# Attention inputs of a decoder trunk on one core: from stationary weight tiles to token-major rows with moving weights, in nine blocks

## The chip, the cores and the metric

The kernel runs on one core of one Trainium2 chip. A core has TensorE (matrix products, from SBUF into PSUM), VectorE (DVE in the rows), ScalarE (ACT), GpSimd (POOL), SyncE (SP, here the issuer of nearly all loads) and 16 DMA engines. The time is that of the device for one execution, in microseconds (us); the number compared is the median over runs.

## The reference

One batch of 256 tokens, model width 2048, two layers: a sparse-attention mixer and a short convolution, each followed by a SwiGLU FFN (hidden width 5632). All is fp32. The change lies in the first mixer:

```python
def _dsa_mixer(h, w_in, q_norm, k_norm, w_out):
    proj = h @ w_in                       # columns: q 2048, k 512, v 512, qi 1024, ki 64, wi 16
    q, k, v, qi, ki, wi = jnp.split(proj, ATTN_SPLITS, axis=-1)
    ...
    q = _rope(_rmsnorm(q, q_norm), cos_h, sin_h)      # 16 heads of 128
    k = _rope(_rmsnorm(k, k_norm), cos_h, sin_h)      # 4 heads of 128
    qi = _rope(qi, cos_i, sin_i)                      # 16 index heads of 64
    ki = _rope(ki, cos_i, sin_i)[:, :, 0, :]
    ...
    rel = jax.nn.relu(jnp.einsum('bqhd,bsd->bqhs', qi_b, ki).astype(jnp.float32))
    idx_score = jnp.einsum('bqhs,bqh->bqs', rel, wi_b.astype(jnp.float32))
    idx_score = jnp.where(causal, idx_score, -jnp.inf)
    _, sel = lax.top_k(idx_score, topk)               # 64 keys of each query
    ...                                               # softmax over the selected keys, grouped heads
    return o @ w_out
```

`h` is the RMS norm of x over the 2048 columns. The rotation of a head takes its halves x1 and x2 to x1 cos - x2 sin and x2 cos + x1 sin, with angles by token position.

## The kernel before

**Precision and slots.** Each fp32 matrix is split into a high part (rounded to the fp32r type) and a low rest, and a product is the sum high x high + high x low + low x high. Weights come in slots of 128 x 1024 numbers: SP loads a slot into `stage`, ScalarE copies it to `w_hi` (L1006), VectorE subtracts to get `w_lo` (L1393), TensorE uses both. `w_hi` and `w_lo` hold four slots (RING), so ScalarE may split slot n once TensorE has finished slot n-4. In the attention part `stage` is used four deep too, later eight deep (DEEP). Normed activations lie token-last in `xs` (and `hs` for head outputs and FFN hiddens): 128 features on partitions, 256 tokens, high then low.

**Order.** There is no scheduler: each engine has a program of its own, written slot by slot, and after certain slots come extra steps (the dictionaries `{slot: [steps]}`; `steps_between` walks them). Engines meet only by semaphores. An engine takes its instructions in order, so a step that waits holds up the weight splits behind it.

**Attention inputs.** Function `stream` keeps a 128x128 weight tile stationary and moves `xs`: the high tile against high and low activations (512 columns, L520), the low tile against the high ones (256 columns, L525). The result is feature-major: 128 features on partitions, 256 tokens in two halves of a bank, which ScalarE and VectorE add (`take_cross` L1012, `qkv_sum` L1594) and scale by the token's norm, broadcast over partitions (L1596). The stages:
- the first block: x arrives in four column parts, is transposed on TensorE (`turn_x`, L584), and the index key with the head weights (80 columns) and the first 256 index columns are multiplied along with it;
- three index blocks of 256 columns. A rotation of halves is a product with a constant matrix on TensorE (`qi_turn` L628, `ki_turn` L614 to L617); scores are L640, their sums over heads L1551, then eight rounds of top-8 and replace on VectorE (L1567, L1570);
- four groups g, each with k and v of one kv head (four slots) and its four query heads (eight slots). On TensorE `turn_kvq` has the mean of k squared (L668), the rotation of k (L670), the turn of v (L672) and the rotation of two query heads (L676); `turn_q23` the other two (L683); `vars_q` sixteen products with one column (L692) for the mean squares of the queries. GpSimd multiplies by the cosine (`cos_products`, L1981 and L1983), VectorE by the sine (L1601, L1613) and adds. Then come logits (L702), softmax (exps L1162, `normalise` L1644), turns of the probabilities (L711) and outputs (L717 to L722), in the next group.

**Output projection.** `stream_rows` (L549 to L551) moves the weights, 512 columns, against stationary 128x128 tiles of `hs`: the result is token-major. Four blocks j of eight slots; each is added to the residual `res`, and the steps of the next norm run between the slots (`norm_steps`). The head-3 group's logits, softmax and outputs run in the first block. The FFN that follows (L774 to L776) and all after it use the same slot machinery; there GpSimd issues DMAs that add one weight block to another (L1994).

## Time and profile before

| | us |
|---|---|
| median of 3 runs | 2097.96 |
| lowest, highest | 2097.86, 2098.32 |
| the profiled execution, from its first to its last instruction (span) | 2096.4 |
| TensorE busy | 2081.3 (99%) |
| VectorE busy | 1725.3 (82%) |
| ScalarE busy | 1177.2 (56%) |
| GpSimd busy | 118.3 (6%) |
| first weight product starts | 13.2 |
| first product of the FFN starts | 349.4 |

The profile is one execution, taken by the hardware. Its own time is the span of 2096.4 us with 1.6 us around it, against the median. A row of a timeline gives start and duration of one or several like instructions; products overlap, so TensorE's pace is read from the distance between starts and not from the duration. "PE" is TensorE's products, "PEld" its weight loads, which run beside them. "a <- b" is the tile written and the tiles read. A wait names the engine that ended it.

### The profile page before, as it was taken

How to read it: one execution, taken by the hardware profiler on the slowest of the kernel's cores; microseconds unless marked ns; L12 is line 12 of the kernel's file. 1: busy time of each engine (PE TensorE's matmuls, PEld its weight loads, DVE VectorE, ACT ScalarE, POOL GpSimd, SP SyncE). 2: the span in 40 equal slices, each digit the busy share in tenths (PEclk: the TensorE clock that was granted, in tenths of full speed). 3: DMA queues.
4: the chain of work that ended last, by engine and by line, in shares of the span. 5: the costliest groups of instructions: out<-in, count | busy, mean ns of one | idle time of the engine just before them, and what ended most of it. 6: DMA issues, size and time to landing. Idle time of an engine off the chain costs nothing.

```text
span 2096.4 us, 28772 instructions
## 1 busy us (share of the span) xinstructions
PE 2081.3 (99%) x9675; PEld 1729.7 (83%) x9675; DVE 1725.3 (82%) x1968; ACT 1177.2 (56%) x1428; POOL 118.3 (6%) x131
## 2 busy tenths in 40 slices
PE   8999999999999999999999999999999999999999
PEld 7888878788888888888888888888888888888887
DVE  5887757999999997876788877579999999978666
ACT  5456555665566564554465555466655665645443
POOL 0001000001000000000000000000010000000000
PEclk9999999999999999999999999999999999999999
DMA  7555456777777777667667666567777777767674
GB/s 230 152 145 152 158 171 192 223 224 227 228 226 220 231 219 215 216 202 215 211 196 211 204 203 196 190 196 222 224 226 229 225 221 230 221 213 216 204 220 147
DMA packets 251616, 432.33 MB, mean 206 GB/s; under 512 B 16912, under 2 KB 58000, under 8 KB 251536
## 3 DMA queue, kind: packets, MB, share of 16 engines
q1 hardware_dynamic: 233824, 399.23, 58.8%
q0 software_dynamic: 16848, 30.68, 8.7%
q10 hardware_dynamic: 864, 1.37, 0.2%
q8 instruction: 49, 0.80, 0.2%
q14 instruction: 31, 0.25, 0.0%
HBM read 429.12 MB, written 2.10 MB: 206 GB/s over the span
## 4 chain that ended last, share of the span: by engine, by line
PE 96%; DVE 2%; ACT 1%; issue 1%; DMA 0%; ACTq 0%; DVEq 0%; SPq 0%
PE ps L774 24%; PE ps L776 24%; PE ps L775 24%; PE ps L520 6%; PE ps L551 4%; PE ps L549 4%; PE ps L550 4%; PE ps L525 3%; PE ps L584 2%; DVE w_lo L1393 1%; PE ps L702 0%; PE ps L640 0%; ACT w_hi L1006 0%; PE ps L711 0%; PE ps L692 0%
## 5 line engine op out<-in xcount | busy, mean ns | idle before, releaser
L1393 DVE TENSOR_TENSOR w_lo<-stage,w_hi 128x1024 fp32r<-128x1024 f32 x748 | 902.3, 1222 | 232.4 <-ACT w_hi L1006 228.4
L1006 ACT ACTIVATE w_hi<-stage 128x1024 fp32r<-128x1024 f32 x748 | 772.7, 1055 | 536.6 <-PE ps L776 365.5
L774 PE MATMUL ps<-w_hi,xs 128*128 128x512 f32 x1122 | 439.4, 392 | 0.3
L776 PE MATMUL ps<-w_hi,xs 128*128 128x512 f32 x1122 | 437.0, 389 | 0.0
L775 PE MATMUL ps<-w_lo,xs 128*128 128x512 f32 x1122 | 436.6, 389 | 0.0
L774 PEld LDWEIGHTS ps<-w_hi,xs 128*128 128x128 f32 x1122 | 210.6, 188 | 44.3 <-DVE gated L1699 1.1
L776 PEld LDWEIGHTS ps<-w_hi,xs 128*128 128x128 f32 x1122 | 210.6, 188 | 44.1
L775 PEld LDWEIGHTS ps<-w_lo,xs 128*128 128x128 f32 x1122 | 210.7, 188 | 42.9
L774 PE MATMUL ps<-w_hi,hs 128*128 128x512 f32 x584 | 227.6, 390 | 0.0
L776 PE MATMUL ps<-w_hi,hs 128*128 128x512 f32 x584 | 227.2, 389 | 0.0
L775 PE MATMUL ps<-w_lo,hs 128*128 128x512 f32 x584 | 227.2, 389 | 0.0
L520 PE MATMUL ps<-xs,w_hi 128*128 128x512 f32 (+1 forms) x528 | 170.7, 406 | 0.0
L1246 ACT ACTIVATE t_hi<-t_raw 128x1024 fp32r<-128x1024 f32 x117 | 123.8, 1058 | 76.3 <-DVE t_raw L1735 45.2
L1742 DVE TENSOR_TENSOR t_lo<-t_raw,t_hi 128x1024 fp32r<-128x1024 f32 x117 | 142.9, 1222 | 17.5 <-ACT t_hi L1246 17.5
L1735 DVE TENSOR_TENSOR t_raw<-stage,t_raw 128x1024 f32<-128x1024 f32 x117 | 142.7, 1220 | 0.0
L1994 POOL DMA_DIRECT2D stage<-in_w_gate x86 | 75.7, 881 | 1034.1 <-DMA stage<-in_w_up 833.5
L776 PEld LDWEIGHTS ps<-w_hi,hs 128*128 128x128 f32 x584 | 109.6, 188 | 22.8
L774 PEld LDWEIGHTS ps<-w_hi,hs 128*128 128x128 f32 x584 | 109.6, 188 | 22.7
L775 PEld LDWEIGHTS ps<-w_lo,hs 128*128 128x128 f32 x584 | 109.6, 188 | 22.5
L1242 ACT ACTIVATE t_hi<-t_raw 128x512 fp32r<-128x512 f32 x117 | 73.4, 627 | 95.3 <-PE ps L776 67.2
L525 PEld LDWEIGHTS ps<-xs,w_lo 128*128 128x128 f32 (+1 forms) x528 | 96.8, 188 | 21.4
L525 PE MATMUL ps<-xs,w_lo 128*128 128x256 f32 (+1 forms) x528 | 103.2, 280 | 0.0
(226 smaller groups left out, 2824.7 us busy)
## 6 DMA issues: line engine op xcount, KB each, us to landing
stage<-in_w_gate SPq DMA_DIRECT2D x176, 512.0 KB, 4.0
stage<-in_w_up SPq DMA_DIRECT2D x176, 512.0 KB, 4.9
stage<-in_w_down SPq DMA_DIRECT2D x176, 512.0 KB, 4.9
stage<-in_conv_w_in SPq DMA_DIRECT2D x96, 512.0 KB, 4.8
stage<-in_attn_w_in SPq DMA_DIRECT2D x48, 512.0 KB, 3.8
stage<-in_w_gate POOLq DMA_DIRECT2D x86, 256.0 KB, 5.6
stage<-in_attn_w_out SPq DMA_DIRECT2D x32, 512.0 KB, 4.8
stage<-in_conv_w_out SPq DMA_DIRECT2D x32, 512.0 KB, 4.8
```

The source lines that it names most:

```text
L520: return pe.matmul(ps[0:count, banks[m], :], w_hi[:, slot, at], rhs, start=k == 0, stop=last)
L525: return pe.matmul(ps[0:count, banks[m], TOK:], w_lo[:, slot, at], rhs[:, 0:TOK], start=False, stop=False)
L549: pe.matmul(bank, hi, w_hi[:, slot, cols], start=k == 0, stop=False)
L550: pe.matmul(bank, hi, w_lo[:, slot, cols], start=False, stop=False)
L774: pe.matmul(ps[:, bank, :], hi, b_hi, start=start, stop=False)
L775: pe.matmul(ps[:, bank, :], hi, b_lo, start=False, stop=False)
L776: return pe.matmul(ps[:, bank, :], lo, b_hi, start=False, stop=stop)
L1006: nc.scalar.activation(w_hi[:, j % RING, :], stage[:, at, :], ACT.Copy).then_inc(hi_done, 1)
L1246: nc.scalar.activation(t_hi[:, 0:2, :], t_raw[:, 0:2, :], ACT.Copy).then_inc(t_high, 1)
L1393: tt(w_lo[:, p, :], stage[:, stage_at(first + j), :], f32(w_hi[:, p, :]), ALU.subtract).then_inc(lo_done, 1)
L1735: tt(t_raw[:, 0:2, :], left, bcast(t_raw[:, 2, :], 2), ALU.subtract).then_inc(t_step, 1)
L1742: tt(t_lo[:, 0:2, :], t_raw[:, 0:2, :], f32(t_hi[:, 0:2, :]), ALU.subtract).then_inc(t_ready, 1)
```

## The change

The attention inputs are computed token-major, in nine blocks of eight slots (`FRONT`): block 0 has the last four index heads, the index key and the head weights (336 columns), blocks 1 and 2 six index heads each (384), block 3 all of k, block 4 all of v, blocks 5 to 8 four query heads each (512). A slot has 256 rows of a block. The 128x128 activation tiles are stationary and the weights move, six products per 128 rows.

- The norm's factor is one number per token and partition, applied by ScalarE as it evicts a block into `rows` (`evict`).
- Rotation on rows: GpSimd multiplies by the cosine table (`cos`), VectorE multiplies the swapped halves by the signed sine table (`swap`), and VectorE (index blocks, `index_add`) or GpSimd (k and q, `head_add`) adds. The head norms' gains are multiplied into the tables once, on GpSimd (`head_tables`). k is scaled by its inverse norm on GpSimd.
- Mean squares of heads come from ScalarE's squares with an accumulator (`head_squares`, eight small ones for each of k and the four query blocks).
- Each rotated block is transposed on TensorE (`index_turn`, `turn_k`, `turn_q`) and copied out by ScalarE. v needs no turn.
- The matrices for means and rotations go; the tables are token-major, and their five loads are issued by GpSimd after the last part of x.
- `stage` is eight deep throughout, x comes in five parts, a table load for ScalarE stands at the start, and the loops over blocks are written out.
- In the output projection the slots of the first two column blocks are interleaved (`AO_SLOTS`), so that rows of late heads come late, and the norm steps move with it.

GpSimd's queue before, from its first product to the loop's end (`s_made`, `k_gained`, `q_gained` are semaphores of TensorE and ScalarE):

```order
L1981 TENSOR_TENSOR kr<-k_gn,tab 128x256 [waits k_gained,in_small]
L1983 TENSOR_TENSOR qr<-gated,tab 128x1024 [waits q_gained]
L1985 UNCONDITIONAL_BRANCH
L1985 ISA
L1980 REGISTER_ALU [waits k_gained]
L1981 TENSOR_TENSOR kr<-k_gn,tab 128x256 [waits s_made]
L1982 REGISTER_ALU
L1983 TENSOR_TENSOR qr<-gated,tab 128x1024 [waits q_gained]
```

GpSimd's queue in the changed kernel, up to the first query block's sum (`sums` and `cross` are the buffers of the rotated rows and of the swapped products; `front_taken` is an eviction, `index_turned` and `k_turned` are TensorE's turns):

```order
L1920 TENSOR_TENSOR sums<-rows,tab_i 128x2x320 [waits front_taken,in_small]
L1905 TENSOR_TENSOR tab_k<-tab_h,hgain 128x256 x2
L1905 TENSOR_TENSOR tab_q<-tab_h,hgain 128x256 x2
L1920 TENSOR_TENSOR sums<-rows,tab_i 128x2x384 [waits index_turned,front_taken] x2
L1920 TENSOR_TENSOR sums<-rows,tab_k 128x1024 [waits index_turned,front_taken,tab_made]
L1927 TENSOR_TENSOR sums<-sums,cross 128x1024 [waits front_swapped,front_cos]
L1940 TENSOR_TENSOR sums<-sums,k_inv 128x1024 [waits front_roped,k_inverse]
L1920 TENSOR_TENSOR sums<-rows,tab_q 128x1024 [waits k_turned,front_taken]
L1927 TENSOR_TENSOR sums<-sums,cross 128x1024 [waits front_swapped,front_cos]
```

What was four pairs of products became eight products over the blocks, four for the tables, five sums and one scaling; each waits for an eviction or a turn, and TensorE's turns wait for them.

TensorE before, at the end of a head group and where the next begins:

```order
L668 MATMUL ps<-k_sq,mat_a 128x256 [waits k_squared,rel_done]
L670 MATMUL ps<-k_gn,mat_a 128x256 [waits k_gained]
L672 MATMUL ps<-mat,raw 128x128 x2
L676 MATMUL ps<-gated,mat_a 128x256 [waits q_gained]
L676 MATMUL ps<-gated,mat_a 128x256
```

TensorE in the changed kernel, in block 6 after its third slot, where the first query block is turned (`mat` is the identity):

```order
L584 MATMUL ps<-w_lo,xs 128x512
L585 MATMUL ps<-w_hi,xs 128x512
L618 MATMUL ps<-mat,sums 128x128 [waits kr_ready,front_roped]
L618 MATMUL ps<-mat,sums 128x128 x7
L583 MATMUL ps<-w_hi,xs 128x512 [waits lo_done]
```

The means and rotations by constant matrices are gone; one wait on the summed rows, and eight turns, stand in the place of a group's matrix work.

VectorE in the changed kernel, second and third block, around the first index turn's input:

```order
L1480 TENSOR_TENSOR cross<-rows,tab_i 128x2x5x32 [waits in_small,front_taken]
L1480 TENSOR_TENSOR cross<-rows,tab_i 128x2x5x32
L1360 TENSOR_TENSOR w_lo<-stage,w_hi 128x768 [waits hi_done] x2
L1488 TENSOR_TENSOR sums<-sums,cross 128x2x320 [waits front_swapped,front_cos]
L1491 COPY sums<-sums 128x2x64 [waits front_roped]
L1360 TENSOR_TENSOR w_lo<-stage,w_hi 128x768 [waits hi_done] x3
```

The copy ends what TensorE's first index turn waits for; two weight splits stand ahead of the sum.

The code, cut to what the steps below speak of:

```diff
+FRONT = ((D + 2 * KV * HD + 12 * ID, 4 * ID + ID + IH), (D + 2 * KV * HD, 6 * ID), (D + 2 * KV * HD + 6 * ID, 6 * ID),
+         (D, KV * HD), (D + KV * HD, KV * HD), *((g * REP * HD, REP * HD) for g in range(KV)))
+KI_AT = 4 * ID
+WI_AT = KI_AT + ID
+K_BLOCK, V_BLOCK, Q_BLOCK = 3, 4, 5
+FRONT_SLOTS = KT // 2
+
+S_AO = len(FRONT) * FRONT_SLOTS
+AO_SLOTS = (*((j, s) for j in range(2) for s in range(4)), *((j, s) for j in range(2) for s in range(4, 6)),
+            *((j, s) for j in range(2) for s in range(6, 8)), *((j, s) for j in range(2, 4) for s in range(8)))
+AO_DONE = tuple(S_AO + AO_SLOTS.index((j, FRONT_SLOTS - 1)) + 1 for j in range(4))
+AO_NORM = (14, 18, 24)
...
+            sp.dma_start(mat.ap(), ident).then_inc(in_ident, 16)
+            load_x(x_part(0), in_x[0])
+            load_front(0, 0)
+            load_x(x_part(1), in_x[1])
+            load_front(0, 1)
+            for j in range(1, 4):
+                load_x(slice(WIDE * j, WIDE * (j + 1)), in_x[j + 1])
+                load_front(0, 2 * j)
+                load_front(0, 2 * j + 1)
+            for b in range(1, len(FRONT)):
+                for s in range(FRONT_SLOTS):
+                    load_front(b, s)
+            for at, (j, s) in enumerate(AO_SLOTS):
+                load(S_AO + at, at % DEEP, attn_w_out[s * 2 * P:(s + 1) * 2 * P, WIDE * j:WIDE * (j + 1)], WIDE)
 
             def load_wide(first, w, tiles):
...
+            def front_slot(b, s):
+
+                width = FRONT[b][1]
+                slot = s % RING
+                if s == 0 and b >= 2:
+                    pe.wait_ge(front_taken, 2 * (b - 1))
+                if b == 0:
+                    x_low_done(pe, s)
+                pe.wait_ge(lo_done, FRONT_SLOTS * b + s + 1)
+                for kk in range(2):
+                    k = 2 * s + kk
+                    cols = slice(kk * width, (kk + 1) * width)
+                    for a in range(2):
+                        bank = ps[:, FRONT_BANKS[b % 2][a], 0:width]
+                        hi, lo = half(xs, k, a)
+                        pe.matmul(bank, hi, w_hi[:, slot, cols], start=k == 0, stop=False)
+                        pe.matmul(bank, hi, w_lo[:, slot, cols], start=False, stop=False)
+                        mm = pe.matmul(bank, lo, w_hi[:, slot, cols], start=False, stop=k == KT - 1)
+                mm.then_inc(slot_used, 1)
+
...
+            def index_turn(b):
+
+                if b == 0:
+                    pe.wait_ge(index_added, 1)
+                else:
+                    pe.wait_ge(front_roped, b + 1)
+                    pe.wait_ge(rel_done, b)
+                for m in range(3):
+                    for a in range(2):
+                        at = TOK * (m % 2) + P * a
+                        mm = pe.transpose(ps[:, 6 + m // 2, at:at + P], roped[:, a, P * m:P * (m + 1)], IDENT)
+                mm.then_inc(index_turned, 1)
...
+            steps = {(1, 4): [lambda: index_turn(0)], (1, 6): [lambda: score_heads(0)],
+                     (2, 3): [lambda: index_turn(1)], (2, 5): [lambda: score_heads(1)],
+                     (3, 3): [lambda: index_turn(2)], (3, 5): [lambda: score_heads(2)],
+                     (3, 7): [lambda: score_heads(3)], (4, 5): [turn_k]}
+            for p in range(KV):
+                at = Q_BLOCK + 1 + p
+                steps = merged(steps, {(at, 2): [lambda p=p: turn_q(p)], (at, 3): [lambda p=p: logits(p)],
+                                       (at + 1, 0): [lambda p=p: turn_prob(p)], (at + 1, 1): [lambda p=p: outputs(p)]})
+            for h in range(3):
+                turn_x(h)
+            for b in range(len(FRONT)):
...
+            def evict(b):
+
+                act.wait_ge(slot_used, FRONT_SLOTS * (b + 1))
+                if b == 0:
+                    act.wait_ge(first_rs, 1)
+                elif b != V_BLOCK:
+                    act.wait_ge(front_swapped, rope_no(b))
+                    act.wait_ge(front_cos, rope_no(b))
+                dst = v_rows if b == V_BLOCK else rows
+                for a in range(2):
+                    nc.scalar.activation(dst[:, a, 0:FRONT[b][1]], ps[:, FRONT_BANKS[b % 2][a], 0:FRONT[b][1]],
+                                         ACT.Copy, scale=rs[:, 0, a:a + 1]).then_inc(front_taken, 1)
+
+            def head_weights():
...
+            steps = {(1, 0): [lambda: x_square(0, 0)], (1, 1): [lambda: x_square(0, 1)],
+                     (1, 2): [lambda: x_square(1, 0)], (1, 3): [lambda: x_square(1, 1)],
+                     (1, 4): [first_root_step], (1, 5): [lambda: evict(0), head_weights],
+                     (2, 0): [lambda: index_copy(0)], (2, 2): [lambda: relu(0)], (2, 3): [lambda: evict(1)],
+                     (2, 7): [lambda: index_copy(1)], (3, 1): [lambda: relu(1)], (3, 3): [lambda: evict(2)],
+                     (3, 7): [lambda: index_copy(2)], (4, 1): [lambda: relu(2)],
+                     (4, 3): [lambda: evict(K_BLOCK)], (4, 4): [lambda: relu(3), k_squares], (4, 5): [root_k],
+                     (5, 1): [copy_k], (5, 3): [lambda: evict(V_BLOCK)]}
+            for p in range(KV):
+                at = Q_BLOCK + 1 + p
+                steps = merged(steps, {(at, 3): [lambda p=p: evict(Q_BLOCK + p)], (at, 4): [lambda p=p: q_squares(p)],
+                                       (at, 5): [lambda p=p: root_q(p)], (at, 6): [lambda p=p: copy_q(p)],
+                                       (at + 1, 0): [lambda p=p: exps(p, 0)], (at + 1, 1): [lambda p=p: exps(p, 1)],
...
+            def swap(b):
+
+                dve.wait_ge(front_taken, 2 * b + 2)
+                if b == 0:
+                    dve.wait_ge(in_small, 80)
+                elif b == K_BLOCK:
+                    dve.wait_ge(tab_made, 4)
+                if rope_no(b):
+                    dve.wait_ge(front_roped, rope_no(b))
+                if b == 1:
+                    dve.wait_ge(index_added, 1)
+                dim = rope_heads(b)[1]
+                src = by_head(rows, b)
+                dst = by_head(swapped, b)
+                sin = rope_table(b)[:, 1, :, :]
+                for side in range(2):
+                    to, of = (slice(dim // 2 * s, dim // 2 * (s + 1)) for s in (side, 1 - side))
...
+            steps = {(1, 0): [set_score], (1, 3): [first_sum], (1, 4): [first_scale], (1, 5): [lambda: swap(0)],
+                     (1, 7): [lambda: index_add(0)], (2, 2): [lambda: add_scores(0)], (2, 3): [lambda: swap(1)],
+                     (2, 5): [lambda: index_add(1)], (3, 1): [lambda: add_scores(1)], (3, 3): [lambda: swap(2)],
+                     (3, 5): [lambda: index_add(2)], (4, 1): [lambda: add_scores(2)], (4, 3): [lambda: swap(K_BLOCK)],
+                     (4, 4): [lambda: add_scores(3), bound_scores], (4, 5): [invert_k],
+                     (4, 7): [lambda: top_rounds((0,))]}
+            steps = merged(steps, {(5, j): [lambda j=j: top_rounds((j + 1,))] for j in range(7)}, {(5, 7): [make_mask]})
+            for p in range(KV):
+                at = Q_BLOCK + 1 + p
+                steps = merged(steps, {(at, 3): [lambda p=p: swap(Q_BLOCK + p)], (at, 7): [lambda p=p: logit(p)],
+                                       (at + 1, 1): [lambda p=p: normalise(p, 0)],
...
+            pool.wait_ge(in_x[4], 16)
+            for dst, src in ((tab_i, tables_i), (tab_h, tables_h), (hgain, head_gains), (bound, bounds), (taps, conv_taps)):
...
+            cos(0)
+            head_tables(tab_k, 2)
+            head_tables(tab_q, 0)
+            cos(1)
+            cos(2)
+            pool.wait_ge(tab_made, 4)
+            cos(K_BLOCK)
+            head_add(K_BLOCK)
+            pool.wait_ge(k_inverse, 1)
+            pool.wait_ge(front_roped, rope_no(K_BLOCK) + 1)
+            inverse = k_inv[:, :, :].unsqueeze(3).to_broadcast([P, 2, KV, HD])
+            nc.gpsimd.tensor_tensor(by_head(roped, K_BLOCK), by_head(roped, K_BLOCK), inverse, ALU.mult).then_inc(k_ready, 1)
+            for p in range(KV):
+                cos(Q_BLOCK + p)
+                head_add(Q_BLOCK + p)
 
```

## Rows read from the trace of the kernel before

**Rows 1.** The page, part 4: the chain that ended last, by engine.
```profile
PE 96%; DVE 2%; ACT 1%; issue 1%; DMA 0%; ACTq 0%; DVEq 0%; SPq 0%
```

**Rows 2.** Windows of three stages, us; the first line names the columns.
```profile
core 0: us, PE busy (x) PEld busy (x) DVE busy (x) ACT busy (x) POOL busy (x), PEclk, DMA share, GB/s
13.20:32.50 19.30, 19.30 (x108) 16.00 (x106) 11.59 (x21) 14.92 (x28) 0.00 (x0) 0.91 0.83 247
...
74.10:248.10 174.00, 173.64 (x1008) 149.00 (x1006) 134.47 (x223) 100.38 (x161) 12.66 (x7) 1.00 0.52 154
248.10:349.40 101.30, 99.75 (x464) 81.99 (x463) 67.29 (x81) 57.33 (x90) 3.39 (x2) 1.00 0.53 169
```

**Rows 3.** Waits of TensorE in 0 to 350 us: total, times, longest.
```profile
PE ps L584 <- DMA res<-in_x: 6.3, 1, 6.3
PE ps L584 <- DVE xs L1418: 2.4, 1, 2.4
PE ps L711 <- DVE prob L1644: 1.4, 1, 1.4
```

**Rows 4.** The start: chain, timeline (start, length), DMA rate to 30 us.
```profile
1.33 4.85 DMA res<-in_x
...
8.34 1.28 ACT L1032 ACT_TABLE_LOAD   x1 [8.34 <-PE ps L584]
...
13.22 0.67 PE L520 MATMUL ps<-xs,w_hi 128*80 128x512 f32 x1
...
GB/s 0 0 89 165 210 218 292 374 335 364 397 370 361 324 339 363 378 412 389 415 399 343 300 319 333 316 331 231 141 341 253 41 191 365 175 270 322 105 232 330
```

**Rows 5.** Timeline of TensorE: products of a head group, then of the projection.
```profile
205.81 0.62 PE L520 MATMUL ps<-xs,w_hi 128*128 128x512 f32 x2
206.27 0.40 PE L525 MATMUL ps<-xs,w_lo 128*128 128x256 f32 x2
206.50 0.63 PE L520 MATMUL ps<-xs,w_hi 128*128 128x512 f32 x2
...
262.92 0.39 PE L551 MATMUL ps<-w_hi,hs 128*128 128x512 f32 x1
263.15 0.39 PE L549 MATMUL ps<-w_hi,hs 128*128 128x512 f32 x1
```

**Rows 6.** The chain of 0 to 360 us in order: small groups.
```profile
56.77 0.87 PE ps L628 x4
...
209.45 0.87 PE ps L683 x4
210.32 1.68 PE ps L692 x16
...
289.75 0.87 PE ps L584 x8
```

**Rows 7.** Timelines of GpSimd (three rows) and of VectorE (two).
```profile
103.59 0.74 POOL L1981 TENSOR_TENSOR kr<-k_gn,tab 128x256 f32<-128x256 f32 x1 [102.58 <-ACT k_gn L1127]
117.77 3.41 POOL L1983 TENSOR_TENSOR qr<-gated,tab 128x1024 f32<-128x1024 f32 x1 [13.44 <-ACT gated L1140]
...
162.92 2.39 POOL L1983 TENSOR_TENSOR qr<-gated,tab 128x1024 f32<-128x1024 f32 x1 [12.88 <-ACT gated L1140]
...
163.75 1.84 DVE L1605 TENSOR_TENSOR kr<-kr,k_sq 128x256 f32<-128x256 f32 x1
165.63 0.42 DVE L1608 TENSOR_TENSOR kr<-kr,k_rt 128x256 f32<-128x256 f32 x1
```

**Rows 8.** Timeline of ScalarE: first exp, and the split after the eighth.
```profile
136.42 0.40 ACT L1162 ACTIVATE prob<-prob,npeak 128x128 f32<-128x128 f32 x1
...
139.95 2.00 ACT L1006 ACTIVATE w_hi<-stage 128x1024 fp32r<-128x1024 f32 x2
```

**Rows 9.** The page, parts 5 and 6: GpSimd DMA issues and landing.
```profile
L1994 POOL DMA_DIRECT2D stage<-in_w_gate x86 | 75.7, 881 | 1034.1 <-DMA stage<-in_w_up 833.5
...
stage<-in_w_gate POOLq DMA_DIRECT2D x86, 256.0 KB, 5.6
```

885 lines of the change are left out of this document (351 added, 534 removed).

## The prediction

> **What bounds the kernel now.** I read the chain that ended last first: 96% of it is TensorE [rows 1]. So time goes only where TensorE's own work gets shorter, or a wait of TensorE goes; what VectorE, ScalarE, GpSimd or the DMAs save is worth nothing by itself. The second view is the table of stages [rows 2]. The change touches the stretch from 0 to 349.4 us: the first block (13.2 to 32.5), the index blocks (to 74.1), the four head groups (to 248.1) and the output projection (to 349.4). What follows, 1747 us, runs the same instructions. The third is TensorE's waits [rows 3]: 8.7 us at the start; behind it TensorE is idle for 174.0 - 173.64 = 0.4 us in the head groups and 101.3 - 99.75 = 1.5 in the projection [rows 2], 1.9 in all. DMA is at half to two thirds of its share in the stretch, the clock at its full level after the first block [rows 2]. The whole sum is therefore one over TensorE's queue from 0 to 349.4 us, plus the waits that the new order makes.
>
> **Start.** Today the first weight product starts at 13.2 us [rows 4]. Ahead of it stand the landing of x's first 512 KB (1.33 + 4.85 us), 16 turns of x (two column blocks), a table load of 1.28 us on ScalarE that nothing hides, and the splits. Afterwards the table is loaded ahead, and x's first part is halved. But TensorE's queue holds three turns of x ahead of the first product, and the third needs the second column block, behind 64 + 256 + 344 + 256 + 344 + 512 KB = 1.78 MB. With 0.58 MB ahead, the first 512 KB landed at 6.2 us; 1.2 MB more at 0.3 to 0.37 MB per us (row of GB/s) is 9.4 to 10.2 us. Four turns follow, about 0.8 us (at most twice their later 0.11 each): first product at 10.3 us, **-2.9 us** (from -4.5, if data comes faster, to -1).
>
> **Weight products.** Today one 128x128 weight tile costs a 512- and a 256-column product. Four of these (two tiles) start every 0.69 to 0.70 us, 0.349 us a tile [rows 5]; 33 tiles (the 80-column one costs the same) times 16 rows are 184.3 us. Afterwards the weights move: per 128 rows and block six products of the block's width. A 512-column product is shown in the output projection: 0.2275 us from start to start [rows 5]; six blocks of 96 are 576 x 0.2275 = 131.0 us. Widths 384 and 336 no row shows. The nearest are 512 (0.2275) and 256 (0.116, half of the 0.23 that a pair of low products takes); on the line between them they are 0.172 and 0.151 us: 192 x 0.172 + 96 x 0.151 = 47.5 us. Bounds: no gain from narrowness (0.2275 each) is +18 us, strictly by columns without the 0.005 us of offset -1. I take the line, since 256 and 512 lie on it. Sum 178.5: **-5.8 us**. It is small, as the columns streamed are nearly the same.
>
> **Small products.** These lie on TensorE in full, and here the gain is [rows 6]. Gone: four rotations of index queries (L628, 0.87 each, 3.5), the index key (two products of that size and two turns, 1.1) and the statistic (two of half the size, 0.4); in each of four head groups the key's mean and rotation (two products as in L628, 0.86, so 3.4), the value's two turns (0.9 in all), the query rotations (L676 as L683, 0.86 each, 6.9) and the means of the squares (L692, 1.68, so 6.7). Together 23.0 us. Added: 18 index turns and 40 head turns; a turn is 0.109 us (L584, eight in 0.87): 6.3 us. Scores, logits, probability turns and outputs stay. Twelve more turns of x fall behind the first product: +1.3. **-15.4 us**. Of the 349.4 us, the parts priced here and those that stay leave some 3 us over; I put it on the 33 places where TensorE turns from small groups back to weights, 0.1 us each. 24 places remain: **-1.0 us** (0 to -2).
>
> **The output projection.** 32 slots before and after, same products. Reordering lets eight slots run before head 2's output is needed and twelve before head 3's. Today logits, softmax and outputs of the last heads leave the 1.5 us of idle, nearly all in one wait of 1.4 [rows 3]. ScalarE's and VectorE's norm steps move from slots 12 to 18. Slot 16 then waits for an addition that VectorE makes behind split 17; it has slots 14 and 15, 5.4 us, for two splits and 1.2 us of sum. Worth nothing beyond the waits below.
>
> **New waits: the term that decides.** Weight splits on ScalarE (1.06) and VectorE (1.22, for 1024 elements) stand in the same in-order queues as the steps, and may run three slots ahead of TensorE. A turn after slot n that needs a step queued behind split n+3 has one slot (2.06 us at width 384) for split, split and step.
> - First index turn: it stands after slot 4 of the second block, its sum on VectorE behind split 7. Split 0.8, split 0.95, sum and copy 1.1 = 2.9 against 2.06: 0.8 us late, always.
> - In this place GpSimd makes a product and four tables. Today's rows show what it does to VectorE [rows 7]: the sum of two SBUF operands took 1.84 us in place of 0.42 while GpSimd's product ran, to 0.3 us past its end, and another such product took 3.41 in place of 2.39. So they exclude each other. Four tables of 0.74 us can each slip between VectorE's splits: up to +3.0. I take +2.2, since not all of them meet the four operations in question.
> - Second index turn: two slots of lead, but 3.3 us of score sums and GpSimd's 1.8 us product in them: 0.9. Third: two wide slots, 0.
> - Key turn: ScalarE's eviction, eight squares, root, then GpSimd's 2.4 us scaling, in six slots: 0.5. First query turn: eviction (split 1.06, 1.1), two GpSimd products of 2.39 [rows 7] with a 1.3 us VectorE product between them, 7.2 against 8.2 us; any one exclusion overdraws it: 0.7. Later ones have 3.5 us more, from the probability turns and outputs in between.
> - Per head: ScalarE needs 8 splits (8.5), an eviction 1.1, exps 3.5 (eight from 136.42 to 139.95), squares as many and at most as much, two tables 2.6 [rows 4, 8], copies 1.1 + 1.6 + 1.1 (1024, 1536 and 1024 elements at a split's rate) and a root 0.3, together 23.3 us in a block where TensorE has 8 x 2.73 + 7 = 29 us. Probability turns are due 0.5 to 0.9 us after their input is ready, query copies 1.2 us: 1.0 for all four.
> Together 0.8 + 2.2 + 0.9 + 0.5 + 0.7 + 1.0 = 6.1, in place of 1.9: **+4.2 us**. The bounds are 0 to 20 us in all.
>
> On the exclusion, the Trainium skill has the rule: SBUF — State Buffer, section "SBUF: two separate sides", calls the shared port pair an exclusive lock held for a whole instruction, against a VectorE instruction with two SBUF inputs. The trace agrees by the 1.84 us. The rule speaks against this change, which brings GpSimd from 8 products to 18. If it held up every one of these behind VectorE's splits, on top of the waits above, it would be the second rival's time.
>
> **Sum.** -2.9 - 5.8 - 15.4 - 1.0 + 4.2 = **-20.9 us**. The profiled execution's span is 2096.4, its own median 2097.96, so 1.56 us lie around the span and stay. 2096.4 - 20.9 = 2075.5 of span, **2077 us**.
>
> **Rivals.**
> 1. All steps are covered: waits of 1 us in place of 6.1, and a start at 9.5 us: 2071. For it: VectorE is free for a third of the stretch [rows 2]. Against: the first turn's 0.8 us is in the order. 15%.
> 2. GpSimd and VectorE hold each other up: ten more operations of 2.4 us, of which each costs half on a chain with no slack, +12 us: 2089. For it: 3.41 and 1.84 [rows 7]. Against: most have 2 to 4 us of slack. 14%.
> 3. Constants late: GpSimd now issues the five constant loads behind the last part of x, which lands about 16 us; issues of 0.9 and a landing of 5.6 [rows 9] put them at 26 us, against first need at 35. If instead they go one by one, 16 + 5 x 6.5 = 48 us, and the first index turn waits 11 us: 2088. No row shows two loads in flight on that queue. 8%.
> 4. Widths 384 and 336 cost as 512: +18 us, 2095, within 0.2%. 4%.
> 5. Slower: ScalarE becomes the bound of the head blocks. Its in-order queue puts each head's squares, copies and exps between splits; it decides above 29 us a block. If squares and exps cost their two records without overlap and each step waits a slot, it is 23.3 + 11.2 = 34.5 us (sixteen records of 0.19 us, and four waits of half a slot and more), 5.5 us more in each of the blocks with head work (five), on top of 6: 2077 + 27 = 2104. Against: exps overlap today [rows 8]. 6%.
> 6. The end of the projection collides with the FFN's start, +4: 2081, inside the forecast's own range.
>
> **How the numbers follow.** Forecast 53% (2073 to 2083), rivals 1 to 5 15, 14, 8, 4 and 6%. The range leaves out the slower case and the top of rival 4: 2068 to 2092. Faster by over 0.2% (4.2 us, about what can be told from no change): forecast, rivals 1, 2, 3 = 0.90; same 0.04; slower 0.06.
>
> **What would show it.** The first product at 10 us; first FFN product at 328 us in place of 349.4; 512-column products 0.2275 us apart throughout; a wait of about 3 us ahead of the first index turn, named VectorE, and under 1 us elsewhere; GpSimd's 1024-element products above 2.4 us. Wrong would be a wait at every head, idle ScalarE waiting for loads, or a stage beyond 350 us that changes its length.

## The result and the profile after

The changed kernel takes **2078.02 us** by the median (four runs, 2075.32 to 2079.43) against 2098.0 for the kernel before (2097.86 to 2098.32). The ratio is 0.9903, with a 95% interval of 0.9889 to 0.9917. The profiled execution has a span of 2077.5 us and took 2079.43; the two runs next to the median had spans of 2076.0 and 2076.2. TensorE is still 96% of the chain that ended last. The first FFN product starts at 330.55 us, where it was 349.42, so 18.87 us are gone ahead of it. Behind it lie 1746.95 us, as before (1746.98).

Windows of the changed kernel: the first block, blocks 1 and 2, blocks 3 to 8 with the projection's first four slots, and the rest of the projection. The columns are those of [rows 2].

```profile
10.48:29.45 18.97, 18.97 (x118) 18.86 (x117) 12.06 (x21) 12.79 (x25) 2.90 (x5) 1.00 0.94 328
29.45:73.52 44.07, 41.39 (x238) 39.68 (x237) 29.01 (x41) 23.15 (x31) 11.26 (x6) 0.92 0.58 191
73.52:245.79 172.27, 171.15 (x812) 139.28 (x812) 135.77 (x193) 109.25 (x226) 37.01 (x12) 1.00 0.49 161
245.79:330.55 84.76, 84.76 (x390) 69.67 (x389) 54.06 (x68) 49.21 (x79) 1.28 (x2) 1.00 0.53 169
```

Behind the first block DMA, VectorE and ScalarE are as far from full as before (in it the DMA share is 0.94, where [rows 2] had 0.83); the granted clock of the second window is 0.92, where [rows 2] had 1.00 behind the first block. That is the first thing that the forecast did not have. TensorE's waits up to 330 us (total, times, longest), in answer to [rows 3]:

```profile
PE ps L549 <- DMA res<-in_x: 7.5, 3, 4.4
PE ps L598 <- DVE sums L1491: 2.7, 1, 2.7
PE ps L618 <- POOL sums L1927: 1.1, 1, 1.1
```

Behind the start there are two, 2.7 us ahead of the first index turn and 1.1 us ahead of the first query turn. The wait of 1.4 us ahead of the probability turns is gone.

TensorE's timeline at the start, then pairs of neighbouring products of 336, 384 and 512 columns, in answer to [rows 4, 5]:

```profile
9.72 1.12 PE L549 MATMUL ps<-mat,res 128*128 128x128 f32 x4 [1.96 <-DMA res<-in_x]
10.48 0.63 PE L583 MATMUL ps<-w_hi,xs 128*128 128x336 f32 x1
10.91 0.48 PE L584 MATMUL ps<-w_lo,xs 128*128 128x336 f32 x1
11.19 0.48 PE L585 MATMUL ps<-w_hi,xs 128*128 128x336 f32 x1
...
15.22 0.32 PE L583 MATMUL ps<-w_hi,xs 128*128 128x336 f32 x1
15.37 0.32 PE L584 MATMUL ps<-w_lo,xs 128*128 128x336 f32 x1
...
37.94 0.33 PE L584 MATMUL ps<-w_lo,xs 128*128 128x384 f32 x1
38.12 0.33 PE L585 MATMUL ps<-w_hi,xs 128*128 128x384 f32 x1
...
76.97 0.39 PE L583 MATMUL ps<-w_hi,xs 128*128 128x512 f32 x1
77.19 0.39 PE L584 MATMUL ps<-w_lo,xs 128*128 128x512 f32 x1
```

The first product comes at 10.48 us. The pace, from start to start, is 0.28 us at first, and later 0.15 for 336 columns, 0.17 for 384 and 0.23 for 512 (the mean over neighbouring products of a width at full pace is 0.154, 0.174 and 0.227). The chain's groups of six index turns and eight key turns, in answer to [rows 6]:

```profile
84.61 0.66 PE ps L598 x6
...
116.27 0.88 PE ps L618 x8
```

Around the first index turn (VectorE, then GpSimd, then TensorE):

```profile
35.62 2.27 DVE L1480 TENSOR_TENSOR cross<-rows,tab_i 128x320 f32<-128x320 f32 x2
37.81 2.90 DVE L1360 TENSOR_TENSOR w_lo<-stage,w_hi 128x768 fp32r<-128x768 f32 x2
40.64 1.34 DVE L1488 TENSOR_TENSOR sums<-sums,cross 128x640 f32<-128x640 f32 x1
42.01 0.63 DVE L1491 COPY sums<-sums 128x128 f32<-128x128 f32 x1
```

```profile
35.74 1.81 POOL L1920 TENSOR_TENSOR sums<-rows,tab_i 128x640 f32<-128x640 f32 x1 [11.62 <-ACT rows L1046]
37.50 2.40 POOL L1905 TENSOR_TENSOR tab_k<-tab_h,hgain 128x256 f32<-128x256 f32 x2
39.86 2.70 POOL L1905 TENSOR_TENSOR tab_q<-tab_h,hgain 128x256 f32<-128x256 f32 x2
```

```profile
42.70 1.54 PE L598 MATMUL ps<-mat,sums 128*128 128x128 f32 x6 [2.68 <-DVE sums L1491]
43.89 0.67 PE L583 MATMUL ps<-w_hi,xs 128*128 128x384 f32 x1
44.36 0.52 PE L584 MATMUL ps<-w_lo,xs 128*128 128x384 f32 x1
44.68 0.52 PE L585 MATMUL ps<-w_hi,xs 128*128 128x384 f32 x1
...
49.00 0.34 PE L584 MATMUL ps<-w_lo,xs 128*128 128x384 f32 x1
49.18 0.34 PE L585 MATMUL ps<-w_hi,xs 128*128 128x384 f32 x1
```

TensorE has slot 4's last product at 39.68 us. The sum of the rotated rows ends at 42.0 and its copy at 42.6. VectorE's four operations ahead of the turn (two splits, the sum, the copy) all lie beside GpSimd's tables (37.5 to 42.6 us). And behind the turn the products of 384 columns are 0.32 us apart, up to 48.7 us; then they are 0.17 to 0.18 apart again.

The first query turn's input, VectorE's swap and GpSimd's product and sum:

```profile
146.73 3.50 DVE L1480 TENSOR_TENSOR cross<-rows,tab_q 128x512 f32<-128x512 f32 x2
...
146.78 2.91 POOL L1920 TENSOR_TENSOR sums<-rows,tab_q 128x1024 f32<-128x1024 f32 x1 [32.23 <-ACT rows L1046]
150.38 3.23 POOL L1927 TENSOR_TENSOR sums<-sums,cross 128x1024 f32<-128x1024 f32 x1 [0.69 <-DVE cross L1480]
```

The two start together and take 3.50 and 2.91 us, where the swap takes 1.28 by itself (all_four, at 142.58 us) and GpSimd's product of this size took 2.39 [rows 7]. The sum, which comes to GpSimd while VectorE is at a split, takes 3.23 us.

### The profile page after: what moved, and what is told of

Read it like the earlier page. It is cut to its first block, busy times and chain, and to the rows that moved or that the text cites. A ratio compares the mean times of both kernels' runs of the same rounds, so it can differ in the third digit from the quotient of the medians.

```text
span 2077.5 us, 27665 instructions
## 1 busy us (share of the span) xinstructions
PE 2061.7 (99%) x9395; PEld 1713.1 (82%) x9395; DVE 1708.2 (82%) x1914; ACT 1178.1 (57%) x1487; POOL 154.4 (7%) x146
## 4 chain that ended last, share of the span: by engine, by line
PE 96%; DVE 2%; ACT 1%; issue 1%; DMA 0%; POOL 0%; SPq 0%; ACTq 0%; DVEq 0%; POOLq 0%
PE ps L723 24%; PE ps L724 24%; PE ps L725 24%; PE ps L523 3%; PE ps L521 3%; PE ps L522 3%; PE ps L583 3%; PE ps L585 3%; PE ps L584 3%; PE ps L537 2%; PE ps L687 1%; PE ps L688 1%; PE ps L689 1%; PE ps L642 1%; DVE w_lo L1347 0%
## 5 line engine op out<-in xcount | busy, mean ns | idle before, releaser
L1347 DVE TENSOR_TENSOR w_lo<-stage,w_hi 128x1024 fp32r<-128x1024 f32 x688 | 832.0, 1223 | 224.2 <-ACT w_hi L952 220.6
L952 ACT ACTIVATE w_hi<-stage 128x1024 fp32r<-128x1024 f32 x688 | 710.0, 1054 | 491.6 <-PE ps L725 364.7
L1360 DVE TENSOR_TENSOR w_lo<-stage,w_hi 128x1024 fp32r<-128x1024 f32 (+2 forms) x72 | 89.4, 1246 | 42.7 <-ACT w_hi L1008 42.5
L583 PE MATMUL ps<-w_hi,xs 128*128 128x512 f32 (+2 forms) x288 | 111.2, 386 | 0.0
L1008 ACT ACTIVATE w_hi<-stage 128x1024 fp32r<-128x1024 f32 (+2 forms) x72 | 70.3, 977 | 69.2 <-PE ps L585 69.1
```

The costliest lines, as they stand in the source:

```text
L583: pe.matmul(bank, hi, w_hi[:, slot, cols], start=k == 0, stop=False)
L952: nc.scalar.activation(w_hi[:, j % RING, :], stage[:, at, :], ACT.Copy).then_inc(hi_done, 1)
L1347: tt(w_lo[:, p, :], stage[:, stage_at(first + j), :], f32(w_hi[:, p, :]), ALU.subtract).then_inc(lo_done, 1)
L1360: tt(w_lo[:, p, 0:w], stage[:, stage_at(n), 0:w], f32(w_hi[:, p, 0:w]), ALU.subtract).then_inc(lo_done, 1)
```

## Experiments

after_again is the changed kernel once more, the other eleven are edits of it; each was timed in five rounds beside the kernel before. "TensorE's stretch" is from its first weight product to its first FFN product in the profiled execution; it leaves out the start and what lies behind. "Low" is how long TensorE ran at the lower pace from the first index turn on. The kernel before was timed 30 times in these rounds and lay between 2096.32 and 2099.19: it scatters by 2.9 us too, more than its first four runs showed.

| kernel | median us | lowest to highest | stretch us | wait, index turn | low us | wait, query turn |
|---|---|---|---|---|---|---|
| changed | 2078.02 | 2075.32 to 2079.43 | 320.07 | 2.7 | 6.0 | 1.1 |
| after_again | 2078.01 | 2075.70 to 2079.50 | 318.62 | 2.7 | 2.9 | 1.1 |
| tables_first | 2074.79 | 2074.31 to 2075.10 | 315.18 | 1.0 | 0 | 1.1 |
| turn_later | 2074.23 | 2073.84 to 2074.41 | 314.81 | 0.6 | 0 | 1.1 |
| start_two | 2076.63 | 2075.32 to 2076.75 | 319.47 | 2.7 | 2.9 | 1.1 |
| all_four | 2072.70 | 2071.89 to 2073.23 | 315.89 | 0 | 0 | 1.3 |
| add_on_vector | 2075.18 | 2074.22 to 2076.62 | 317.67 | 2.7 | 3.1 | 0 |
| turn_sooner | 2080.55 | 2079.98 to 2081.34 | 321.75 | 4.7 | 5.8 | 1.1 |
| turns_twice | 2080.29 | 2079.95 to 2082.64 | 321.16 | 2.7 | 0 | 1.1 |
| joined_vector | 2069.91 | 2069.31 to 2071.03 | 312.57 | 0 | 0 | 0 |
| joined_early | 2071.17 | 2071.05 to 2072.17 | 313.90 | 0 | 0 | 0 |
| ao_short | 2077.35 | 2077.13 to 2079.68 | 318.38 | 2.7 | 0 | 1.1 |
| joined_twice | 2075.16 | 2074.11 to 2075.57 | 317.94 | 0 | 0 | 0 |

**The changed kernel once more.**

> The changed kernel once more, as the yardstick of this set and to see its scatter: its four times so far lie from 2075.3 to 2079.4 us where the kernel before keeps within 0.5 us. Theory (clock): the wait of 2.7 us ahead of the first index turn is at the edge of what lets the granted clock fall to its lower level, and the products behind it (43.9 to 48.8 us) run at 0.32 us in place of 0.174. Then the time is about 2078 with a scatter of some us. Rival: the scatter was chance, and it is 2078 within 0.5.

The median is the same and so is the scatter: eight runs within 4.2 us. One row each of the granted clock, over 6.0 us from the first index turn on: the changed kernel, this repetition, and turns_twice, which does up to this place the same instructions:

```profile
42.70:48.70 6.00, 6.00 (x21) 6.00 (x22) 0.81 (x1) 1.33 (x2) 0.00 (x0) 0.50 0.27 100
```

```profile
42.70:48.70 6.00, 5.94 (x29) 5.94 (x30) 1.57 (x3) 1.66 (x2) 0.00 (x0) 0.76 0.31 112
```

```profile
42.00:48.00 6.00, 5.97 (x43) 5.68 (x45) 1.80 (x2) 2.49 (x3) 0.00 (x0) 1.00 0.32 115
```

PEclk (the number behind the five engines) is 0.50, 0.76 and 1.00. In the first, TensorE ran at 1.2 GHz for all of the 6.0 us; in the second for half of it; in the third not at all. The wait ahead was 2.68 us in all three. So one and the same wait lets the clock fall or not from run to run, and for a different time. At 0.32 us in place of 0.174 a product, 6.0 us at the lower level cost 2.8 us. From the first index turn to the second the first takes 19.96 us, the second 18.43 and the third 17.12, for the same instructions: the low clock cost 2.8, 1.3 and 0 us. The spans of the first two differ by the same 1.5 us (2077.5 and 2076.0): the scatter between these two is the clock's.

**Tables ahead of the first product.**

```diff
-            cos(0)
             head_tables(tab_k, 2)
             head_tables(tab_q, 0)
+            cos(0)
```

> GpSimd makes its four head tables ahead of its first cosine product, in its idle time from 29 to 35.7 us, and not between the two blocks' products. Theory (exclusion, then clock): VectorE's split, sum and copy behind the first swap (1.49, 1.28 and 0.64 us beside the tables) fall to about 0.96, 0.8 and 0.3; the wait ahead of the first index turn falls from 2.7 to 1.3 us, the clock stays at its upper level, and with it some 2.7 us of slow turns and products go: about 2074. Rival 1 (the order alone makes the wait): the wait stays at 2.7 and the time at 2078. Rival 2 (shorter wait, but the clock falls as before): 2076.5.

VectorE's last operations ahead of the turn, and TensorE's wait:

```profile
38.01 1.81 DVE L1360 TENSOR_TENSOR w_lo<-stage,w_hi 128x768 fp32r<-128x768 f32 x2
39.75 0.81 DVE L1488 TENSOR_TENSOR sums<-sums,cross 128x640 f32<-128x640 f32 x1
40.59 0.23 DVE L1491 COPY sums<-sums 128x128 f32<-128x128 f32 x1
...
PE ps L598 <- DVE sums L1491: 1.0, 1, 1.0
```

Two splits 1.81 us (2.90 beside the tables), sum 0.81 (1.34), copy 0.23 (0.63): 2.0 us less for the same four instructions, while the swap beside the cosine product stays at 2.28. The wait is 1.0 us and the clock stays at its upper level. The median falls by 3.2 us: 1.7 of wait, the rest clock. The theory of the exclusion holds in size (I had put 2.2 us of the wait on it), and the two rivals, that the order alone makes the wait and that the clock falls all the same, do not.

**The first index turn one slot later.**

```diff
-            steps = {(1, 4): [lambda: index_turn(0)], (1, 6): [lambda: score_heads(0)],
+            steps = {(1, 5): [lambda: index_turn(0)], (1, 6): [lambda: score_heads(0)],
```

> TensorE makes the first index turn after slot 5 of the second block in place of slot 4; nothing else changes. Theory: TensorE fills 2.08 us with the slot's products, the wait falls from 2.7 to 0.6 us and the clock stays up: 2.1 + 2.7 = 4.8 us less, about 2073, and the scatter of the changed kernel goes. Rival (the wait only moves: the split of the slot behind it is late too, since ScalarE stands at the copy of the turn): no gain, 2078. Rival 2 (the low clock is no result of the wait): the wait falls, 12 products at 0.32 us stay, 2076.

```profile
PE ps L598 <- DVE sums L1491: 0.6, 1, 0.6
```

A wait of 0.6 us is left of 2.7 (the slot fills 2.1), no product runs slow, and the median is 3.8 us lower. The four runs lie within 0.6 us, where the changed kernel's lie within 4. Of two separate ways to shorten the wait both give more than the wait itself, and both end the scatter.

**The first index turn one slot sooner.**

```diff
-            steps = {(1, 4): [lambda: index_turn(0)], (1, 6): [lambda: score_heads(0)],
+            steps = {(1, 3): [lambda: index_turn(0)], (1, 6): [lambda: score_heads(0)],
```

> The first index turn one slot sooner, after slot 3 of the second block, which makes the wait ahead of it longer by one slot's products: 2.7 + 2.1 = 4.8 us. Theory (an idle stretch of that size lets the granted clock fall, once, for a stretch whose length varies from run to run by some 3 us and doesn't grow with the wait): 2080.1, scatter as in the changed kernel. Rival (the low clock grows with the idle time): slow products for 8 us and more, 2082 or more. Rival 2 (the wait ends no later, since the sum behind split 7 needs that slot's end): under 0.5 us.

```profile
PE ps L598 <- DVE sums L1491: 4.7, 1, 4.7
```

The wait is 4.7 us and the time 2080.55, by 2.5 us longer where the theory had 2.1. The products of 384 columns that are 0.32 us apart are no more than in the changed kernel's profile, fourteen against fifteen. All five runs lie within 1.4 us, as if all had the penalty; only one of them was profiled. Over all profiles here the clock fell behind the wait of 4.7 us (one profile), behind that of 2.7 us in four of six, and behind one of 1.4 us or less never, the first block left aside.

**Two turns of x ahead of the first slot.**

```diff
-            for h in range(3):
+            for h in range(2):
                 turn_x(h)
...
-                    if b == 0 and s + 3 < 8:
-                        turn_x(s + 3)
+                    if b == 0:
+                        for h in ((2, 3) if s == 0 else (s + 3,)):
+                            if h < 8:
+                                turn_x(h)
```

> Two turns of x stand ahead of the first slot in place of three; turns three and four follow behind that slot. Theory (the start is the landing of x's third part at 9.7 us and no wait for weights): the first product comes at 8.2 us in place of 10.5, the later parts land long before their use, and the saving stays: 2.3 us less, about 2075.7. Rival 1 (the load queue sets the block's pace: what starts earlier waits later for loads or for ScalarE's copies): under 0.5 us. Rival 2 (the engine starts cold and the idle stretch behind it grows): nothing or a loss of 1 us.

```profile
8.57 0.62 PE L583 MATMUL ps<-w_hi,xs 128*128 128x336 f32 x1 [0.52 <-DVE w_lo L1362]
...
12.07 1.91 PE L549 MATMUL ps<-mat,res 128*128 128x128 f32 x8
13.63 0.50 PE L583 MATMUL ps<-w_hi,xs 128*128 128x336 f32 x1
```

The first product comes at 8.57 us, 1.9 earlier. The new wait of 0.5 us stands directly ahead of it: without the third turn in between, TensorE comes to the first slot before VectorE has split its weights (until 8.4 us). And the third turn is moved, not saved: turns three and four take 1.56 us behind the first slot, at the lower clock, where the fourth alone took 0.69 in the changed kernel. Against after_again, whose clock was low as long behind the index turn, the first FFN product comes 1.0 us earlier; by the medians 1.4 us are left of the 2.3 that I expected. No load was late, so rival 1 is wrong about the cause and the theory was wrong about the size.

**Four edits at once.** The three edits that gained, and this one:

```diff
-                steps = merged(steps, {(at, 3): [lambda p=p: evict(Q_BLOCK + p)], (at, 4): [lambda p=p: q_squares(p)],
+                steps = merged(steps, {(at, 2): [lambda p=p: evict(Q_BLOCK + p)], (at, 4): [lambda p=p: q_squares(p)],
```

> Four edits to the changed kernel at once: tables ahead of the first cosine product, the first index turn after slot 5, two turns of x ahead of the first slot, and ScalarE evicts each query block after split 2 of the next block in place of split 3 (the eviction stands ahead of that split). Theory (each removes its own part of TensorE's idle time): the index wait and the slow products behind it go in full (-4.4 us from 2078.0), the start gives 1.4 as it did alone, the wait of 1.1 us ahead of the first query turn goes: 2071. Rival (the edits collide: an eviction ahead of its split holds up the weights, or the block with the tables comes earlier than its constants): 2073 or more, with a wait of TensorE for w_lo or for the tables.

GpSimd's cosine product and VectorE's split in block 6, and two waits of TensorE:

```profile
139.17 2.40 POOL L1922 TENSOR_TENSOR sums<-rows,tab_q 128x1024 f32<-128x1024 f32 x1 [31.18 <-ACT rows L1048]
...
140.07 2.58 DVE L1362 TENSOR_TENSOR w_lo<-stage,w_hi 128x1024 fp32r<-128x1024 f32 x1 [2.59 <-ACT w_hi L1010]
...
PE ps L618 <- POOL sums L1929: 1.3, 1, 1.3
PE ps L583 <- DVE w_lo L1362: 0.9, 1, 0.9
```

The first two edits take away the same wait and the same low clock, so their gains don't add. All four together give 5.3 us, where 4.4 and 1.4 us were expected of the first three. The fourth gives nothing, and shows the exclusion once more: GpSimd's product runs from 139.17 to 141.57 us, and the split that comes to VectorE at 140.07 ends at 142.65, after 2.58 us in place of 1.23. That is 1.08 us behind the product's end: nearly the whole split stood still until GpSimd was through. The swap waits behind it. The other wait, 0.9 us, stands ahead of the very first product (at 8.30 us), as in start_two.

**The query sums on VectorE.** In `dve` the sum stands behind the swap, in `pool` it goes:

```diff
-                steps = merged(steps, {(at, 3): [lambda p=p: swap(Q_BLOCK + p)], (at, 7): [lambda p=p: logit(p)],
+                steps = merged(steps, {(at, 3): [lambda p=p: swap(Q_BLOCK + p), lambda p=p: query_add(p)], (at, 7): [lambda p=p: logit(p)],
...
                 cos(Q_BLOCK + p)
-                head_add(Q_BLOCK + p)
```

> VectorE makes the sums of the four query blocks right behind its swapped products; GpSimd keeps the cosine products and the key block. Theory (only the first query turn was late, and GpSimd's sum of 3.23 us beside VectorE's split was its cause): the wait of 1.1 us goes, 2076.9; the other blocks had slack and give nothing. Rival (VectorE is the tighter queue; its logits and prob steps come later): new waits of TensorE ahead of the probability turns, 2079 or more.

```profile
PE ps L549 <- DMA res<-in_x: 7.2, 3, 4.4
PE ps L598 <- DVE sums L1491: 2.7, 1, 2.7
```

These are all of TensorE's waits up to 300 us. The query wait is gone and none came in its place. The median is 2.8 us lower, more than 1.1; but this profile's clock was low for 3.1 us and the changed kernel's for 6.0, so the medians of two scattered kernels can't tell the 1.1 from the rest. Against after_again (2.9 us of low clock) TensorE's stretch is 0.95 us shorter, about the wait that is gone.

**Turns twice.**

```diff
-                for h in range(4):
+                for h in (0, 1, 2, 3, 0, 1, 2, 3):
```

> Every turn of a key or query block is made twice (40 turns more, to the same place). It measures the term on which the forecast rests, that small groups lie on TensorE in full and at 0.109 us a turn. Theory: 40 x 0.109 = 4.4 us more, 2082.4. Rival (they lie beside waits that would be there anyway): under 1 us, save for the block with the wait.

The key turns of this kernel, then those of the changed one:

```profile
112.61 1.91 PE L618 MATMUL ps<-mat,sums 128*128 128x128 f32 x16
```

```profile
116.11 1.04 PE L618 MATMUL ps<-mat,sums 128*128 128x128 f32 x8
```

Sixteen turns take 1.91 us and eight 1.04: 0.87 us for eight, 0.109 each. Over the five blocks the starts of these groups and of what follows are 8.38 us apart in sum against 4.01, 4.37 us more, as the theory has it. The medians differ by 2.3 only. The profile tells why they can: this execution had no low stretch at all. It was left open whether the difference was the clock's or the turns' own; the last kernel settles it.

**The joined kernels.** Both have the tables first, the first index turn after slot 5 and the third turn of x in the middle of the first slot. (The wait of 0.9 us that the first of the two expectations puts on the third slot was that of the first slot, as said above.) joined_vector has the sums on VectorE, joined_early has them on GpSimd with the eviction and the swap one split earlier.

```diff
+                    if k == 0 and b == 0:
+                        turn_x(2)
```

> Tables first, first index turn after slot 5, VectorE making the query sums, and a start with two turns ahead, the third in the middle of the first slot (after its first 128 rows) and the fourth behind it. In the kernel with four edits two waits were left: 0.9 us for the third slot's low weights (the third turn stood behind the whole first slot at the low clock) and 1.3 us ahead of the first query turn (VectorE's swap stood behind a split that the earlier eviction had delayed). Theory: both go, no wait over 0.2 us is left after 10 us: 2072.7 - 0.9 - 1.3 = 2070.5. Rival (VectorE late with the logits or probabilities for the sums it now has): a wait ahead of the probability turns, 2072 or more.

```profile
PE ps L583 <- DVE w_lo L1362: 0.3, 1, 0.3
```

> As the last, but the query sums stay on GpSimd, and ScalarE's eviction and VectorE's swap of a query block stand behind split 2 of the next block in place of split 3. Theory (the sum was late only for what stood ahead of it in both queues): the query wait falls from 1.1 to about 0, 2070.5 as well. Rival (GpSimd's 3.23 us sum and the split beside it lengthen each other, wherever they stand): 0.5 to 1.3 us of wait stays, 2071.5.

```profile
PE ps L583 <- DVE w_lo L1362: 0.6, 1, 0.6
```

Neither has a wait ahead of a turn. 2069.91 us is the best of the study, 0.9869 of the kernel before (0.9852 to 0.9885), and 8.1 us under the changed kernel. joined_early is 1.3 us slower: in its profile twelve products of the first block ran at the lower level, in joined_vector's six, and with the turns among them the first block took 19.60 us against 18.52; its wait for `w_lo`, ahead of the first product, is 0.6 against 0.3. Moved by one split, GpSimd's sums were in time as well; the rival that they would still cost 0.5 to 1.3 us by the lock is wrong.

**The projection's slots in two rounds.**

```diff
-AO_SLOTS = (*((j, s) for j in range(2) for s in range(4)), *((j, s) for j in range(2) for s in range(4, 6)),
-            *((j, s) for j in range(2) for s in range(6, 8)), *((j, s) for j in range(2, 4) for s in range(8)))
+AO_SLOTS = (*((j, s) for j in range(2) for s in range(4)), *((j, s) for j in range(2) for s in range(4, 8)), *((j, s) for j in range(2, 4) for s in range(8)))
```

> The projection's slots of the first two column blocks in two rounds (rows 0 to 3 of both, then rows 4 to 7 of both) in place of three, so that the first slot that reads head 3's output is the eleventh and not the thirteenth. Theory: that output is complete 1.5 us after TensorE comes to this slot (VectorE's last difference of the changed kernel ends at 269.5, the eleventh slot starts at 268.0), so TensorE waits once, 1.5 us, and the clock stays up: 2079.5. Rival (the order of slots is worth nothing, as TensorE may fill the time elsewhere): 2078.0.

```profile
PE ps L686 <- DVE hs L1575: 1.4, 1, 1.4
```

The wait is there, 1.4 us at the slot that I named. The median does not show it: 2077.35. The clock stayed up in this profile behind the first index turn, and with a scatter of 4 us in both kernels four runs can't tell 1.4 us. Inconclusive by its time, as expected by its trace. It also bounds what the reordering is worth: with rows 6 and 7 one round earlier TensorE waits 1.4 us, as it did before the change.

**Turns twice, with a steady clock.**

> The joined kernel (query sums on VectorE), with every turn of a key or query block made twice. In the changed kernel the same edit gave 2.3 us by the medians and 4.4 us by the trace (groups of 16 in place of 8), with a scatter of 3 us from the clock between them. Here TensorE has no long wait and the clock no reason to fall. Theory: 40 turns x 0.109 = 4.4 us: 2074.3 within 1 us. Rival (the turns fill time that TensorE would wait anyway, as the medians of the changed kernel suggest): 2072.2 or less.

5.25 us more than joined_vector by the medians (2075.16 and 2069.91), 5.37 by the two stretches. Here again twelve products of the first block ran slow in place of six, and the block took 1.1 us more; the rest of the stretch is 4.3 us longer, for 4.4 expected. So the turns lie on the path in full, and the small difference of turns_twice is put down to the clock: its profile had none of the 2.8 us that the changed kernel's had.

## Why the prediction was right, and where it was not

The forecast was 2077.0 us and the range 2068 to 2092. Its terms against TensorE's starts in the two profiles (from start to start; the gaps ahead of the instructions that waited are taken out of products and groups, and so is what the lower clock behind the index turn cost):

| term | forecast | measured |
|---|---|---|
| start, first product at 10.3 | -2.9 | -2.7 (10.48) |
| weight products, with the places between groups | -5.8 - 1.0 | -5.6 |
| small groups | -15.4 | -15.2 |
| waits behind the start | +4.2 | +1.9 |
| lower clock behind the first index turn | 0 | +2.8 |
| sum up to the FFN | -20.9 | -18.8 |

**Start.** Right, and for the reason given: the third turn of x waits for 1.78 MB, and its data came at 9.7 us, inside the estimate of 9.4 to 10.2. One reading was off without harm: in the kernel before 24 turns stand ahead of the first product, not 16 (the third column block's eight start at 12.39 us); the twelve more behind it are counted right.

**Weight products.** The line between 256 and 512 columns was right: 0.154 and 0.174 us for 336 and 384, against 0.151 and 0.172. The -1.0 for fewer changes between groups was wrong. I had found some 3 us of the kernel before that no row explained and put them on these places. Half of it was the clock. In the kernel before the first 80-column tile's products start 0.64 to 0.68 us from one pair to the next (the first row of it stands in [rows 4]), and a pair later takes 0.349. Two windows of its profile, the turns just ahead and the products:

```profile
12.39:13.20 0.81, 0.81 (x8) 0.81 (x9) 0.81 (x2) 0.81 (x4) 0.00 (x0) 1.00 1.10 406
13.22:16.60 3.38, 3.38 (x13) 2.56 (x12) 3.38 (x7) 3.38 (x9) 0.00 (x0) 0.52 1.03 385
```

The granted clock is 0.52 for 3.4 us, some 1.7 us of loss. The changed kernel has a slow stretch at its start too (0.28 us for 336 columns, twelve times, and a turn), so nothing of it was there to gain. In this profile the row of the granted clock reads 1.00 there, although the pace is half; the pace is what counts.

**Small groups.** -15.2 for -15.4, all on TensorE's path: turns_twice by its trace and joined_twice by its time show 0.109 to 0.11 us a turn.

**Waits.** The place and the size of the first index turn's wait came as forecast (2.7 for 3.0), and so did the first query turn's (1.1 for 0.7). Those that I had put on the second index turn (0.9), the key turn (0.5) and the heads (1.0) are not there. Their slack was enough: GpSimd's products of 1024 elements took 2.9 to 3.45 us and its sums 3.2 to 3.3, where a product had taken 2.39, one product of 768 even took 4.44 (at 56.46 us), and no turn behind the first of each kind waited.

**The step that failed** is "-2.9 ... + 4.2": a wait was priced by its own length. TensorE's wait of 2.7 us at the first index turn let its clock fall to 1.2 GHz, and the six turns behind it took 1.19 us in place of 0.63 and fifteen products 0.32 us each in place of 0.174. In the profiled execution that cost 2.8 us, in others 1.3 to 1.5 or nothing; turn_later and tables_first show it, each with a gain larger than the wait it took away (3.8 for 2.1, 3.2 for 1.7). The forecast came within 1 us of the median by luck in this part: the waits that did not come (2.3 us) and the clock that did nearly cancel.

**The exclusion.** Of the four tables' effect 2.2 us were forecast; VectorE's four operations were 2.0 us shorter without them, and the wait 1.7. The Trainium skill (SBUF — State Buffer, section "SBUF: two separate sides") has the whole instruction excluded; by that rule the trace agrees, most plainly in all_four: a split of 1.23 us took 2.58 and ended 1.08 us behind GpSimd's product. As the cause of a larger loss, rival 2, it did not decide: of 18 operations of GpSimd only those at the first index and the first query turn reached TensorE.

**The other rivals.** The end of the projection against the FFN's start: not seen, the stretch behind the first FFN product is as long as before (1746.95 and 1746.98 us). All covered (2071): wrong as the change stands, but joined_vector, with the two waits and the early start mended, is at 2069.9. Constants late: GpSimd did pause for 4.93 us between its third and fourth load, which I had not foreseen, but its wait in tables_first ended at 29.5 us, ahead of the first need at 35.7. Narrow blocks at the price of wide ones: wrong, by the pace. ScalarE as the bound: not seen; TensorE waited for ScalarE nowhere.

What decides between the executions with and without the fall stays open, and so does how short a wait can be enough. The kernel before gave a hint that the prediction passed over: its slow stretch at 13.22 us stands behind the wait of 2.4 us in [rows 3] and eight turns at full pace. No experiment tested that place, so its cause is not shown. Behind the first block no run here has a wait between 1.4 and 2.7 us.

## What to carry to other kernels

Price a wait of TensorE by two numbers: its length, and the slow products behind it, which came here after 2.7 us in four profiles of six. One slot of distance more, or work on GpSimd moved to where VectorE is idle, took away both here. When a kernel's runs scatter by microseconds, read the granted clock behind its longest wait before comparing medians, and take more than four runs of the old kernel too before calling it steady; two kernels that both scatter can be compared by the starts in their traces. And when a sum over rows leaves microseconds unexplained, look for their place before giving them a name.

## What was not expected of the hardware

- After the same wait of 2.68 us TensorE ran at 1.2 GHz for 6.0 us, for 2.9 to 3.1 us (three kernels) or not at all (two kernels). After 4.7 us it was 5.8 us. After 1.4 us and less the products behind were at full pace in all profiles, the first block left aside.
- At the start the slow products of the first block were six in joined_vector, twelve in joined_early and joined_twice, whose first block has the same order, and ten to fifteen in the others. The Trainium skill (TensorE: Matmul & The Clock Gate, section "Part 1: The HAM clock gate") says that this number changes from run to run, and that one should not reckon with a certain count; the rows agree. The first block took 1.1 us more in joined_early than in joined_vector.
- A VectorE instruction of 1.23 us that met GpSimd's 2.40 us product took 2.58, VectorE's swap of 1.28 us took 3.50 beside GpSimd's cosine product in the query blocks, and GpSimd's product of 2.4 us took up to 3.45: both engines lose, according to who began.
